# VectorE's order at a head's end in a two-layer hybrid attention block: the last score tile's normalisation placed before the next head's copies

## The chip, the cores and the metric

One Trainium2 chip, one of its cores. The whole network step is one program. The metric is the device time of one execution in microseconds (us): the median of several runs. A profile of one execution stands beside it.

## What is computed

Two layers, run over two sets of tokens at once: 512 latent tokens and 128 context tokens, 1024 wide. Everything is in float32. From the reference, cut to what matters here:

```python
def layer(x, cond, lp, cache=None, ropes=None):
    ...
    h = rmsnorm(x, lp['norm1']) * (1 + sc1) + sh1
    proj = h @ lp['w_in']
    ...
    y_a = gb * conv3(gc * xa, lp['conv_a'])
    ...
        y_b = blocked_attention((q_mla_rot, q_mla_raw), (k_l, k_x), (v_l, v_x), MLA_SCALE)
        y_c = blocked_attention((group_heads(axial_rope(qc, rope64), GQA_KV_HEADS), group_heads(qc, GQA_KV_HEADS)),
                                (axial_rope(kc, rope64), kc_x), (vc, vc_x), ATTN_SCALE)
        y_d = windowed_attention(group_heads(axial_rope(qd, rope64), SWA_KV_HEADS), axial_rope(kd, rope64), vd,
                                 group_heads(qd, SWA_KV_HEADS), kd_x, vd_x, lp['swa_sink'], ATTN_SCALE)
    ...
    y = jnp.concatenate([y_a, y_b, y_c, y_d], axis=-1) @ lp['w_out']
    x = x + g1 * y
    h = rmsnorm(x, lp['norm2']) * (1 + sc2) + sh2
    u = conv3(h @ lp['w_up'], lp['conv_ff'])
    ua, ub = jnp.split(u, 2, axis=-1)
    x = x + g2 * ((jax.nn.silu(ua) * ub) @ lp['w_down'])
    return x, new
```

There are three kinds of softmax attention with 4 heads each. Latent queries attend to the latent keys and to 128 cached ones, context queries to the 128 context keys. One kind sees a window of keys and has a sink, a logit that joins the softmax's denominator. Shift, scale and gate (sh, sc, g) come from a product of the conditioning with `w_ada` (adaLN).

## The kernel before

Each layer runs through the input projection, attention, the output projection and the feed-forward part. Large products are made of three float32r products of high and low halves (`H_hi`, `H_lo` for activations, `W_hi`, `W_lo` for weights). The queues of the five engines are written out by hand and meet at semaphores; an engine works strictly in its own order.

**Attention** goes by heads 0 to 11. Heads 0 to 3 are of the second kind above (y_c), 4 to 7 the windowed one with the sink, 8 to 11 the first kind (y_b). A head has five query tiles of 128: 0 to 3 latent, tile 4 context. `attention_order` (L173) writes one list of steps, and each engine walks it and takes its part:

- `("T", key)`: TensorE transposes something into PSUM bank 4 or 5, in turn, and another engine copies it out (`evac_fill`, L477). Keys of a head ("K", two parts, into `KTR`) and its queries ("Q", two parts, into `QTR`) are copied by VectorE, as are the fills of the first kind's projections ("MT", "MQ", "MV", into `CQ`, `PMG`, `PMS`, `KS`). Probabilities ("P", into `PT`) are copied by ScalarE. A transposition waits until the bank's last content but one has been copied out.
- `("S", h, q)`: TensorE makes the scores of tile q. VectorE takes the maximum (`maximum`, L1821), ScalarE the exponentials and their sum (`PR`, L945), VectorE divides (`normalise_probs`, L1835): a reciprocal and a multiplication of `PR` with it, and before them, in heads 4 to 7, an addition of the sink's term.
- `("V", h, k)`: TensorE multiplies `PT` with the values. When a head's output is complete, ScalarE writes its high half (`H_hi`) and VectorE its low half (`H_lo`, L1873).
- `("ADA", n)`: TensorE multiplies two half blocks of `w_ada`, each of 512 KB, which SyncE's queue brings into one of three buffers (`RW`), loaded again when the block before has been used.

The list interleaves two heads: while head h's scores are made, head h-1's probabilities are transposed and multiplied. Between two heads it reads:

```python
        if h == 0 or kv_of(h) != kv_of(h - 1):
            order += [("T", ("K", kv_of(h), 0)), ("T", ("K", kv_of(h), 1))]
        order += late + [("T", ("Q", h, 0)), ("T", ("Q", h, 1))]
        ...
        order += [("ADA", todo[0])] + t[:1]
        for q in range(NQ):
            order.append(("S", h, q))
            order += t[q + 1:q + 2] + v[q:q + 1]
```

`late` is the last value product of the head before h-1, and `t[:1]` the transposition of head h-1's tile 4, which waits for all five normalisations of that head (`s_norm`). Keys are shared by two heads in heads 0 to 7, so `KTR` is written anew behind heads 1, 3 and 5, and behind 8, 9 and 10. Behind head 7 there are no scores to interleave: the fills of the last group's projections come in, then head 7's transpositions and value products, then keys and queries of head 8. Behind head 11 follow the adaLN result's move and selection ("MOVE", "SEL") and the output projection.

VectorE (L1849 to L1858) normalises a tile one step late: after the maximum of tile q it divides tile q-1. The last tile's turn comes where the list has that head's first "P" transposition. ScalarE makes a tile's exponentials one step late too: those of tile 4 behind the copy of the head before's last probabilities.

Of the kernel before, what the change touches and what calls it, by code (L numbers as in the profile page):

```python
# [29 lines left out]
QT = NLAT // P  # L30
# [206 lines left out]
def by_scalar(key):  # L237

    return key[0] == "P"
# [19 lines left out]
def backbone_program(nc, x_prompt, x_sample, cache_mla_ckv, cache_mla_kpe, cache_gqa_k, cache_gqa_v,  # L259
# [5 lines left out]
    with ctx:  # L265
# [187 lines left out]
        def prob_ap(h, q):  # L453

            c0 = q * (P + NLAT)
            if q == QT:
                return PR[:, h % 2, c0:c0 + P]
            if h // 4 == 1:
                lo, hi = window(h, q)
                return PR[:, h % 2, c0:c0 + P * (1 + hi - lo)]  # L460
            return PR[:, h % 2, c0:c0 + P + NLAT].rearrange("p (b n) -> p b n", n=HALFK)

        def y_parts(k, r0):

            if k == TT:
                return [(r0, 0, CTX0, CTX0 + P)]
            return [(HD * x, QHALF * x, QHALF * x, QHALF * (x + 1)) for x in range(2)]
# [7 lines left out]
        def evac_fill(eng, copy, l, key):  # L476
# [5 lines left out]
            kind = key[0]  # L482
            if kind == "P":
                _, h, k = key
                i = 6 * h + P_SEQ.index(k)
                if i >= 2:
                    values_done(eng, l, i - 2)
                c0, c1 = (0, P) if k == TT else (P * queries(h, k)[0], P * queries(h, k)[1])
                copy(PT[:, i % 2, c0:c1], bank[:, c0:c1]).then_inc(done, 1)
            elif kind == "Q":  # L490
                _, h, part = key
                if h >= 2:
                    eng.wait_ge(s_mm, l * NS_ + NQ * (h - 1))
                c0, c1 = (0, NLAT) if part == 0 else (NLAT, NLAT + P)
                copy(QTR[:, h % 2, c0:c1], bank[:, 0:c1 - c0]).then_inc(done, 1)
            elif kind == "K":
                _, kv, part = key
                if kv >= 2:
                    last = max(h for h in range(HEADS) if kv_of(h) == kv - 2)
                    eng.wait_ge(s_mm, l * NS_ + NQ * (last + 1))  # L500
                c0, c1 = (0, 512) if part == 0 else (512, KEYS)
                copy(KTR[:, kv % 2, c0:c1], bank[:, 0:c1 - c0]).then_inc(done, 1)
            elif kind == "MT":
                i = key[1]
                if i >= 2:
                    eng.wait_ge(tr_mm, l * NFILL + (FILL_AT[("MV", i - 2)] + 1))
                else:
                    eng.wait_ge(rot_q, l * 3 + 2)
                if i < TT:
                    copy(CQ[0:96, i % 2, 0:2, :], bank[0:96, 0:2 * P].rearrange("p (k n) -> p k n", n=P))  # L510
                copy(CQ[:, i % 2, 2, :], bank[:, 2 * P:3 * P]).then_inc(done, 1)
            elif kind == "MQ":
                eng.wait_ge(new_out, l * 96 + 96)
                copy(PMG[:, key[1], 0:384], bank[:, 0:384]).then_inc(done, 1)
            else:
                src = bank.rearrange("p (h n) -> p h n", n=P)
                copy(KS[:, key[1], :, 0:HD], src[:, :, 0:HD])
                eng.wait_ge(new_out, l * 96 + 96)
                eng.wait_ge(raw_q, l * 3 + 2)
                i = key[1]  # L520
                dst = PMG[:, 0:4, 384:384 + HD] if i == PAST else \
                    PMS[:, i, 0:4 * HD].rearrange("p (h n) -> p h n", n=HD)
                copy(dst, src[:, :, HD:P]).then_inc(done, 1)
# [1038 lines left out]
        def _(dve):  # L1562
            v = nc.vector

            def copy(dst, src):
                return v.tensor_copy(dst, src)  # L1566
# [125 lines left out]
            for l in range(DEPTH):  # L1692
# [128 lines left out]
                def maximum(h, q):  # L1821
                    g, j = divmod(h, 4)
                    n = SIDX[(h, q)]
                    dve.wait_ge(s_mm, l * NS_ + (n + 1))
                    mx, nb = ST[:, 0, n % 4:n % 4 + 1], ST[:, 1, n % 4:n % 4 + 1]
                    s = score_ap(h, q, n)
                    v.tensor_reduce(mx, s, mybir.AxisListType.XY if len(s.shape) == 3 else AXX,  # L1827
                                    ALU.max).then_inc(s_max, 1)
                    dve.wait_ge(s_max, l * NS_ + (n + 1))
                    if g == 1:  # L1830
                        v.tensor_scalar(nb, mx, -SCALES[g], SK[:, j:j + 1], ALU.mult, ALU.min).then_inc(s_nb, 1)
                    else:
                        v.tensor_scalar(nb, mx, -SCALES[g], None, ALU.mult).then_inc(s_nb, 1)

                def normalise_probs(h, q):  # L1835
                    n = SIDX[(h, q)]
                    dve.wait_ge(s_exp, l * NS_ + (n + 1))
                    den, rec = ST[:, 2, n % 4:n % 4 + 1], ST[:, 3, n % 4:n % 4 + 1]
                    if h // 4 == 1:
                        dve.wait_ge(s_sink, l * 20 + (n - 20 + 1))  # L1840
                        v.tensor_tensor(den, den, SE[:, n % 4:n % 4 + 1], ALU.add).then_inc(s_den, 1)
                        dve.wait_ge(s_den, l * 20 + (n - 20 + 1))
                    v.reciprocal(rec, den).then_inc(s_rec, 1)
                    dve.wait_ge(s_rec, l * NS_ + (n + 1))
                    pr = prob_ap(h, q)
                    v.tensor_scalar(pr, pr, rec, None, ALU.mult).then_inc(s_norm, 1)  # L1846

                waiting = None
                for e in ORDERS[l]:  # L1849
                    if e[0] == "S":  # L1850
                        maximum(*e[1:])
                        if waiting:
                            normalise_probs(*waiting)
                        waiting = e[1:]
                        continue
                    if e[0] == "T" and e[1][0] == "P" and waiting and waiting[0] == e[1][1]:
                        normalise_probs(*waiting)
                        waiting = None  # L1858
                    if e[0] == "T" and not by_scalar(e[1]):
                        evac_fill(dve, copy, l, e[1])  # L1860
                    elif e == ("PREP", 2):

                        dve.wait_ge(tr_mm, l * NFILL + (FILL_AT[("K", 3, 1)] + 1))
                        for t in range(QT):
                            copy(KS[:, t, :, HD:96],
                                 PMM[:, t, 320:352].rearrange("p (o n) -> p o n", o=1).to_broadcast([P, 4, ROPE]))
                        v.memset(KS[:, PAST, :, HD:96], 0.0).then_inc(rot_k, 1)
                    elif e[0] == "V" and e[2] in (TT, QT):
                        h, k = e[1:]
                        yi, r0, tile = 3 * h + (k != TT), HD * (h % 2), YTILE[h // 4] + h % 4 // 2  # L1870
                        for x, (p0, b0, c0, c1) in enumerate(y_parts(k, r0)):
                            dve.wait_ge(y_hi, l * (3 * HEADS) + (yi + x + 1))
                            v.tensor_tensor(H_lo[r0:r0 + HD, tile, c0:c1], PS[p0:p0 + HD, 6, b0:b0 + c1 - c0],  # L1873
                                            H_hi[r0:r0 + HD, tile, c0:c1].bitcast(F32),
                                            ALU.subtract).then_inc(y_lo, 1)
# [280 lines left out]
```

## Time and profile before

| | us |
|---|---|
| median of 3 runs | 1832.27 (1827.96 to 1833.47) |
| the profiled execution | 1827.39 |
| its span, first to last instruction | 1825.6 |
| busy in it: TensorE matmul | 1714.5 (94%), 11625 instructions |
| VectorE | 1115.0 (61%), 2279 |
| ScalarE | 625.6 (34%), 1257 |
| GpSimd | 148.7 (8%), 152 |
| mean granted TensorE clock | 0.979 of full |

Times are counted from the first instruction. Attention in the first layer lies between 183 and 403, in the second between 1071 and 1281. In the rows, PE is TensorE's matmul, PEld its weight load, DVE VectorE, ACT ScalarE; L12 is line 12 of the kernel. L1106 is every product, L1110 every transposition, L1566 every copy of VectorE, L781 every copy of ScalarE, so a row is told by its tiles: what it writes stands left of the arrow.

### The profile page before, as it was taken

The numbers are of one execution on the slowest core, as the hardware profiler recorded it, in microseconds if no ns is written. First come the engines' busy times: TensorE is split into PE (matmuls) and PEld (weight loads), VectorE is DVE, ScalarE is ACT, GpSimd is POOL, SyncE is SP. The second block draws the span as 40 slices with busy tenths as digits, with TensorE's granted clock in tenths as the row PEclk, the third lists the DMA queues.
The fourth block names the chain that finished last, engine by engine and source line by source line (L and its number), as shares of the span: only waits on it lengthen the run. The fifth ranks groups of instructions, "written<-read, shape, count | busy, mean of one in ns | idle before, by whom it ended". The sixth has DMA issues, their size and how long they took to land.

```text
span 1825.6 us, 30070 instructions
## 1 busy us (share of the span) xinstructions
PE 1714.5 (94%) x11625; PEld 1539.5 (84%) x11625; DVE 1115.0 (61%) x2279; ACT 625.6 (34%) x1257; POOL 148.7 (8%) x152
## 2 busy tenths in 40 slices
PE   5899898899999999999989989878999999999997
PEld 3899554469999999999989965545999999999997
DVE  3656665555765655656782856656477556565675
ACT  2421553453432222232242235435343222222223
POOL 0351100020000000000004402010200000000000
PEclk7999999989999999999999999999999999999998
DMA  8431542332122222222312322212313222222211
GB/s 270 115 96 36 169 138 71 116 105 81 59 81 75 75 71 78 69 80 70 94 49 66 94 77 93 93 42 75 104 56 95 75 76 69 76 74 73 77 58 59
DMA packets 188438, 156.53 MB, mean 86 GB/s; under 512 B 7824, under 2 KB 175284, under 8 KB 188340
## 3 DMA queue, kind: packets, MB, share of 16 engines
q1 hardware_dynamic: 188340, 155.19, 27.7%
q8 instruction: 65, 1.06, 0.2%
q14 instruction: 33, 0.27, 0.1%
HBM read 151.86 MB, written 3.31 MB: 85 GB/s over the span
## 4 chain that ended last, share of the span: by engine, by line
PE 85%; DVE 7%; DMA 2%; ACT 2%; issue 2%; POOL 1%; SPq 0%; DVEq 0%; ACTq 0%
PE PS L1106 81%; PE PS L1110 4%; DMA RW<-in_w_ada_dram 1%; DMA RW<-in_w_in_dram 1%; DVE QTR L1566 1%; DVE H_lo L1873 1%; DVE H_lo L1627 1%; POOL SS L762 1%; ACT H_hi L781 1%; DVE PR L1846 1%; DVE X L1676 0%; POOL W_lo L740 0%; DVE ST L1827 0%; DVE XN_b L1614 0%; ACT PT L781 0%
## 5 line engine op out<-in xcount | busy, mean ns | idle before, releaser
L1106 PE MATMUL PS<-H_hi,W_lo 128*128 128x384 f32 (+1 forms) x1728 | 417.4, 310 | 0.0
L1106 PE MATMUL PS<-H_hi,W_hi 128*128 128x384 f32 (+1 forms) x1728 | 417.3, 310 | 0.0
L1106 PE MATMUL PS<-H_lo,W_hi 128*128 128x384 f32 (+1 forms) x1728 | 417.0, 310 | 0.0
L1106 PEld LDWEIGHTS PS<-H_lo,W_hi 128*128 128x128 f32 x1728 | 276.2, 189 | 0.0
L1106 PEld LDWEIGHTS PS<-H_hi,W_hi 128*128 128x128 f32 x1728 | 275.3, 189 | 1.1 <-issue 1.1
L1106 PEld LDWEIGHTS PS<-H_hi,W_lo 128*128 128x128 f32 x1728 | 276.1, 189 | 0.0
L781 ACT ACTIVATE W_hi<-RW 128x1024 fp32r<-128x1024 f32 (+1 forms) x176 | 183.9, 1049 | 190.0 <-PE PS L1106 161.4
L1942 DVE TENSOR_SCALAR CF<-U,VT 128x644 f32<-128x644 f32 x88 | 49.0, 556 | 268.8 <-ACT U L781 268.5
L1106 PE MATMUL PS<-G_hi,W_hi 128*128 128x384 f32 (+1 forms) x704 | 171.7, 310 | 0.0
L1106 PE MATMUL PS<-G_lo,W_hi 128*128 128x384 f32 (+1 forms) x704 | 171.4, 310 | 0.0
L1106 PE MATMUL PS<-G_hi,W_lo 128*128 128x384 f32 (+1 forms) x704 | 170.6, 308 | 0.0
L781 ACT ACTIVATE U<-PS 128x384 f32<-128x384 f32 (+1 forms) x176 | 67.4, 435 | 288.4 <-PE PS L1106 288.4
L1639 DVE TENSOR_TENSOR W_lo<-RW,W_hi 128x1024 fp32r<-128x1024 f32 x136 | 165.7, 1218 | 0.5 <-ACT W_hi L781 0.4
L1971 DVE TENSOR_TENSOR DN<-PS,DN 128x384 f32<-128x384 f32 (+1 forms) x288 | 122.0, 482 | 19.9 <-PE PS L1106 19.9
L1827 DVE TENSOR_REDUCE ST<-PS 128x1 f32<-128x640 f32 (+3 forms) x120 | 79.6, 664 | 88.5 <-PE PS L1106 88.2
L1106 PE MATMUL PS<-KTR,QTR 128*128 128x320 f32 (+3 forms) x432 | 127.2, 415 | 6.1 <-ACT PR L945 6.1
L1106 PE MATMUL PS<-W_hi,H_hi 128*128 128x256 f32 (+1 forms) x400 | 118.0, 295 | 13.6 <-DVE H_lo L1627 4.3
L781 ACT ACTIVATE PT<-PS 128x128 f32<-128x128 f32 (+2 forms) x144 | 73.2, 508 | 168.3 <-PE PS L1110 168.1
L1106 PE MATMUL PS<-W_lo,H_hi 128*128 128x256 f32 (+1 forms) x400 | 116.8, 292 | 0.0
L1106 PE MATMUL PS<-W_hi,H_lo 128*128 128x256 f32 (+1 forms) x400 | 116.6, 292 | 0.0
L740 POOL TENSOR_TENSOR W_lo<-RW,W_hi 128x1024 fp32r<-128x1024 f32 (+1 forms) x40 | 94.2, 2371 | 249.0 <-ACT W_hi L781 249.0
L1106 PEld LDWEIGHTS PS<-G_hi,W_lo 128*128 128x128 f32 x704 | 113.0, 189 | 0.0
(170 smaller groups left out, 2397.3 us busy)
## 6 DMA issues: line engine op xcount, KB each, us to landing
RW<-in_w_ada_dram SPq DMA_DIRECT2D x96, 512.0 KB, 4.5
RW<-in_w_up_dram SPq DMA_DIRECT2D x88, 512.0 KB, 3.8
RW<-in_w_down_dram SPq DMA_DIRECT2D x44, 512.0 KB, 3.6
RW<-in_w_in_dram SPq DMA_DIRECT2D x28, 512.0 KB, 3.7
RW<-in_w_out_dram SPq DMA_DIRECT2D x16, 512.0 KB, 3.4
RW<-in_w_in_dram SPq DMA_DIRECT2D x8, 352.0 KB, 3.0
out_dram<-OUT SPq DMA_DIRECT2D x5, 512.0 KB, 3.1
XIN<-in_x_sample_dram SPq DMA_DIRECT2D x4, 512.0 KB, 6.6
```

The source lines that it names most:

```text
L740: nc.gpsimd.tensor_tensor(lo[:, 0:width], RW[:, RAW_POS[("w", l, s)] % RAW, 0:width], hi[:, 0:width].bitcast(F32), ALU.subtract).then_inc( ...
L762: nc.gpsimd.tensor_tensor(SS[:, 1, 0:40], SS[:, 0, 0:40], K[:, K_MH:K_MH + 40], ALU.pow).then_inc(hp, 1)
L781: return nc.scalar.activation(dst, src, ACT.Copy)
L1106: return nc.tensor.matmul(out, lhsT, rhs, start=start, stop=stop, skip_group_check=True)
L1110: return nc.tensor.transpose(out, in_, K[0:n, K_ID:K_ID + n])
L1566: return v.tensor_copy(dst, src)
L1627: ins = v.scalar_tensor_tensor(H_lo[:, t, c0:c0 + b1 - b0], XN[x][:, t % 3, b0:b1], MOD[:, 24 * w + t, cond:cond + 1], H_hi[:, t, c0:c0 + ...
L1639: v.tensor_tensor(lo[:, 0:width], RW[:, raw, 0:width], hi[:, 0:width].bitcast(F32), ALU.subtract).then_inc(w_lo, 1)
L1827: v.tensor_reduce(mx, s, mybir.AxisListType.XY if len(s.shape) == 3 else AXX, ALU.max).then_inc(s_max, 1)
L1846: v.tensor_scalar(pr, pr, rec, None, ALU.mult).then_inc(s_norm, 1)
L1942: v.tensor_scalar(CF[:, ch, s, :], U[:, ch, s, 0:T], column(0), None, ALU.mult).then_inc(cv_own, 1)
L1971: ins = v.tensor_tensor(out, piece_bank(2 * t + x, x), out, ALU.add)
```

## The change

In VectorE's walk through the list, when the maximum of tile 4 (`QT`) has been taken and tile 3 divided, tile 4 is divided too, at once.

```diff
@@ -1852,6 +1852,9 @@
                         if waiting:
                             normalise_probs(*waiting)
                         waiting = e[1:]
+                        if e[2] == QT:
+                            normalise_probs(*waiting)
+                            waiting = None
                         continue
                     if e[0] == "T" and e[1][0] == "P" and waiting and waiting[0] == e[1][1]:
                         normalise_probs(*waiting)
```

The lists of the other engines stay as they are. VectorE, at the end of head 1 in the first layer, from tile 3's normalisation to head 2's first maximum, before:

```order
L1843 RECIPROCAL ST<-ST 128x1 [waits s_exp]
L1846 TENSOR_SCALAR PR<-PR,ST 128x640 [waits s_rec]
L1566 COPY KTR<-PS 128x512 [waits tr_mm]
L1566 COPY KTR<-PS 128x256 [waits tr_mm]
L1873 TENSOR_TENSOR H_lo<-PS,H_hi 64x256 [waits y_hi] x2
L1566 COPY QTR<-PS 128x512 [waits s_mm,tr_mm]
L1566 COPY QTR<-PS 128x128 [waits s_mm,tr_mm]
L1843 RECIPROCAL ST<-ST 128x1 [waits s_exp]
L1846 TENSOR_SCALAR PR<-PR,ST 128x128 [waits s_rec]
L1827 TENSOR_REDUCE ST<-PS 128x1 [waits s_mm]
```

and in the changed kernel, where line 1873 has become 1876:

```order
L1843 RECIPROCAL ST<-ST 128x1 [waits s_exp]
L1846 TENSOR_SCALAR PR<-PR,ST 128x640 [waits s_rec]
L1843 RECIPROCAL ST<-ST 128x1 [waits s_exp]
L1846 TENSOR_SCALAR PR<-PR,ST 128x128 [waits s_rec]
L1566 COPY KTR<-PS 128x512 [waits tr_mm]
L1566 COPY KTR<-PS 128x256 [waits tr_mm]
L1876 TENSOR_TENSOR H_lo<-PS,H_hi 64x256 [waits y_hi] x2
L1566 COPY QTR<-PS 128x512 [waits s_mm,tr_mm]
L1566 COPY QTR<-PS 128x128 [waits s_mm,tr_mm]
L1827 TENSOR_REDUCE ST<-PS 128x1 [waits s_mm]
```

The reciprocal and the multiplication of the 128 wide tile, which waits for ScalarE's exponentials (`s_exp`), have moved past the copies of the next keys, the two low halves of y and the copies of the next queries.

TensorE at the same place, in both kernels: the next head's queries, its adaLN products, the transposition of head 1's tile 4 and head 2's first score.

```order
L1110 MATMUL PS<-K,QS 128x128 [waits tr_ev_4]
L1110 MATMUL PS<-K,QS 128x128 x3
L1110 MATMUL PS<-K,QS 128x128 [waits tr_ev_5]
L1106 MATMUL PS<-RW,CT 32x256 [waits raw_in0]
L1106 MATMUL PS<-RW,CT 32x256 x3
L1106 MATMUL PS<-RW,CT 32x256 [waits raw_in1]
L1106 MATMUL PS<-RW,CT 32x256 x3
L1110 MATMUL PS<-K,PR 128x128 [waits s_norm,tr_ev_4]
L1106 MATMUL PS<-KTR,QTR 128x320 [waits tr_ev_4,tr_ev_5,s_exp]
```

Nothing moved here. `s_norm` counts the normalisations, `tr_ev_4` and `tr_ev_5` the copies out of the two banks, `raw_in` the landed weights.

VectorE at the end of head 7, before, from tile 3's normalisation on (the copies between are those of the last group's keys, values and queries):

```order
L1846 TENSOR_SCALAR PR<-PR,ST 128x384 [waits s_rec]
L1566 COPY KS<-PS 128x4x64 [waits tr_mm]
L1566 COPY PMS<-PS 128x256 [waits raw_q,new_out]
L1566 COPY CQ<-PS 128x128 [waits tr_mm]
L1566 COPY PMG<-PS 128x384 [waits new_out,tr_mm]
...
L1867 MEMSET KS 128x4x32
L1841 TENSOR_TENSOR ST<-ST,SE 128x1 [waits s_sink,s_exp]
L1843 RECIPROCAL ST<-ST 128x1 [waits s_den]
L1846 TENSOR_SCALAR PR<-PR,ST 128x128 [waits s_rec]
L1873 TENSOR_TENSOR H_lo<-PS,H_hi 64x256 [waits y_hi] x2
```

In the changed kernel the three rows from `ST<-ST,SE` on stand directly behind the first row, ahead of all of these copies.

## Rows read from the trace of the kernel before

**Rows 1.** Waits of the whole span: who waited for whom: us in total, times, longest.
```profile
PE PS L1110 <- DVE PR L1846: 29.2, 22, 2.7
```
**Rows 2.** Timeline, end of head 1, layer 0: start, us, engine, instruction [idle before].
```profile
204.20 0.20 ACT L945 ACTIVATION_READ_ACCUMULATOR PR<-PS,ST 128x1 f32 x1
204.63 1.02 DVE L1566 COPY KTR<-PS 128x512 f32<-128x512 f32 x2 [0.47 <-PE PS L1110]
205.93 0.88 DVE L1873 TENSOR_TENSOR H_lo<-PS,H_hi 64x256 fp32r<-64x256 f32 x2 [0.28 <-ACT H_hi L781]
206.07 1.07 PE L1106 MATMUL PS<-RW,CT 128*32 128x256 f32 x16
206.84 0.89 DVE L1566 COPY QTR<-PS 128x512 f32<-128x512 f32 x2
207.84 0.29 DVE L1846 TENSOR_SCALAR PR<-PR,ST 128x128 f32<-128x128 f32 x1
208.27 0.30 PE L1110 MATMUL PS<-K,PR 128*128 128x128 f32 x1 [1.13 <-DVE PR L1846]
208.50 1.31 PE L1106 MATMUL PS<-KTR,QTR 128*128 128x320 f32 x4
```
**Rows 3.** Timeline, end of head 2, layer 0.
```profile
221.24 0.88 DVE L1873 TENSOR_TENSOR H_lo<-PS,H_hi 64x256 fp32r<-64x256 f32 x2 [1.14 <-ACT H_hi L781]
222.14 0.89 DVE L1566 COPY QTR<-PS 128x512 f32<-128x512 f32 x2
...
224.22 1.31 PE L1106 MATMUL PS<-KTR,QTR 128*128 128x320 f32 x4
```
**Rows 4.** Timeline, end of head 4, layer 0.
```profile
253.86 0.89 DVE L1566 COPY QTR<-PS 128x512 f32<-128x512 f32 x2
...
255.84 0.89 PE L1106 MATMUL PS<-KTR,QTR 128*128 128x128 f32 x4
```
**Rows 5.** Timeline, end of head 5, layer 0.
```profile
267.30 1.02 DVE L1566 COPY KTR<-PS 128x512 f32<-128x512 f32 x2
...
269.47 0.89 DVE L1566 COPY QTR<-PS 128x512 f32<-128x512 f32 x2
...
271.36 0.89 PE L1106 MATMUL PS<-KTR,QTR 128*128 128x128 f32 x4
```
**Rows 6.** Timeline of TensorE, end of head 0, layer 0.
```profile
191.91 0.64 PE L1106 MATMUL PS<-RW,CT 128*32 128x256 f32 x8 [1.97 <-DMA RW<-in_w_ada_dram]
```
**Rows 7.** Timeline, end of head 8, layer 0.
```profile
341.41 1.01 DVE L1566 COPY KTR<-PS 128x512 f32<-128x512 f32 x2
...
342.84 1.07 PE L1106 MATMUL PS<-RW,CT 128*32 128x256 f32 x16
...
344.27 0.30 PE L1110 MATMUL PS<-K,PR 128*128 128x128 f32 x1 [0.35 <-DVE PR L1846]
```
**Rows 8.** Timeline, end of head 7, layer 0 and layer 1.
```profile
317.38 0.45 PE L1110 MATMUL PS<-K,PR 128*128 128x128 f32 x1 [2.49 <-DVE PR L1846]
...
317.86 0.28 ACT L781 ACTIVATE PT<-PS 128x128 f32<-128x128 f32 x1 [1.02 <-PE PS L1110]
...
318.97 0.78 ACT L781 ACTIVATE H_hi<-PS 64x256 fp32r<-64x256 f32 x2 [0.83 <-PE PS L1106]
...
1203.75 0.28 ACT L781 ACTIVATE PT<-PS 128x128 f32<-128x128 f32 x1 [1.04 <-PE PS L1110]
...
1204.39 0.78 ACT L781 ACTIVATE H_hi<-PS 64x256 fp32r<-64x256 f32 x2 [0.36 <-PE PS L1106]
```
**Rows 9.** Timeline of ScalarE, end of head 11, layer 0.
```profile
391.01 0.28 ACT L781 ACTIVATE PT<-PS 128x128 f32<-128x128 f32 x1 [1.38 <-PE PS L1110]
```
**Rows 10.** Stretches behind heads 7, 11, 11: busy by engine, granted clock, DMA share, GB/s.
```profile
317.30:328.50 11.20, 10.41 (x36) 4.46 (x36) 1.14 (x3) 3.65 (x9) 4.38 (x16) 0.55 0.00 0
390.60:402.70 12.10, 11.35 (x51) 6.71 (x51) 0.30 (x1) 5.80 (x10) 4.66 (x2) 0.58 0.28 88
...
1273.50:1280.90 7.40, 6.76 (x47) 3.91 (x47) 0.29 (x1) 5.48 (x10) 3.99 (x2) 1.00 0.06 8
```

## The prediction

> **What bounds the kernel now.** Heads are numbered 0 to 11, tiles 0 to 4, as in the code; "PE" is TensorE, "DVE" VectorE, "ACT" ScalarE. I read the waits of the whole span first: TensorE's transpositions of PR wait for the PR that VectorE writes 22 times, 29.2 us in all, 2.7 at most [rows 1]. With 12 heads in each of two layers that is one wait per head end but for two. So the question is what else has to be done at a head's end. For that I read the timeline there, engine by engine.
>
> Head 1 [rows 2] is the pattern. The exponential of its last tile is complete at 204.40 (204.20 + 0.20). VectorE copies KTR from 204.63, then H_lo, then QTR until 207.73 (206.84 + 0.89), and only then writes the last PR, complete at 208.13. TensorE's adaLN products end at 207.14; it stands 1.13 us, transposes PR at 208.27 and starts the next head's first score at 208.50. Its order is fixed, so this score stands behind the transposition though it needs only KTR and QTR. The reader is to see that PR could have been ready some 3 us earlier, and that the score, once PR no longer holds it, has QTR to wait for, which ends 0.77 before 208.50. The gain is therefore not the 1.13 of the wait.
>
> **The change, part by part.** No instruction is added or dropped. At every head end the reciprocal and multiplication of tile 4 (with the sink's addition in heads 4 to 7) move ahead of the next head's copies, on VectorE alone; no DMA and no other queue is touched. What is new is that the KTR, H_lo and QTR copies now stand behind a wait for the last exponential, and TensorE's transpositions of the next queries, with the adaLN products behind them, wait for the KTR copies.
>
> Release times I take from [rows 2]: from PR's end, 208.13, to the transposition 0.14; so the score starts 0.15 after the last thing it needs. The moved pair takes 0.47: 0.40 after the QTR copies, and they overlap their end a little; I take 0.5.
>
> *Heads 1, 3, 9 and 10, KTR copies, no sink.* The pair can start at 204.46 and ends at 204.93. The KTR copies were idle 0.47 before they began at 204.63, so they move by 0.3, to an end at 205.96. H_lo began at 205.93 after an idle 0.28, waiting for ACT; that slack swallows nearly all, 0.06 is left. QTR ends at 207.79. The adaLN products end at 207.14 + 0.33 = 207.47, still ahead. The score starts at 207.94 in place of 208.50: 0.56 a head, 8 heads, **4.5 us**.
>
> *Head 2, no KTR copies, no sink.* VectorE was idle 1.14 before H_lo at 221.24 [rows 3], that is from 220.10. In head 1 the exponential ends 0.24 after the third tile's PR; with the same here the pair takes 220.40 to 220.87 and hides entirely. QTR ends at 223.03 as before, the score starts at 223.18, not 224.22: 1.04, two layers, **2.1 us**.
>
> *Heads 4 and 6, no KTR copies, sink.* QTR ends at 254.75, the score started at 255.84 [rows 4]: 0.94 by the same reckoning. With the sink's addition the pair takes 0.65, and head 6 has less room before H_lo; I take 0.85 for the four, **3.4 us**.
>
> *Head 5, KTR copies and sink.* The KTR copies began at 267.30 with no idle time long enough to be listed [rows 5], so they move by about 0.57. Part is swallowed before H_lo, 0.36 reaches QTR: 270.36 + 0.36 + 0.15 = 270.87 in place of 271.36. I take 0.45, two layers, **0.9 us**.
>
> *Heads 0 and 8.* In head 0 TensorE's second adaLN product waited for its weights until 191.91 [rows 6] and ended at 192.55, which the change does not touch: 0. In head 8 KTR begins at 341.41 without a pause, the adaLN products end at 343.91 and the transposition waited only 0.35 more, to 344.27 [rows 7]. The copies move by 0.45, the queries' transpositions and the products with them, to 344.36, and the score starts about when it did: **0**.
>
> *Head 7.* Here 12 more copies and a memset (the next group's keys, values and queries) stood ahead of the pair, and TensorE stood 2.49 [rows 8]. ACT was idle 1.02 before its PT copy and 0.83 before its H_hi copies; in layer 1 it was 1.04 and 0.36. Both waits were for TensorE, which can now transpose as soon as the last product is out. ACT's own copies of QS and KS then come last. The chain on from there (H_lo, the next value product) moves by the sums, 1.85 and 1.40: **3.3 us**.
>
> *Head 11.* The same with ACT idle 1.38 before its PT copy [rows 9]; the later steps follow it one after another. Both layers: **2.8 us**.
>
> The sum is 4.5 + 2.1 + 3.4 + 0.9 + 0 + 3.3 + 2.8 = 17.0 us. Inside a head nothing moves: its first score starts earlier, and the rest follows from it on TensorE. Behind attention the output projection waits for the last value products, so the gain goes through to the end. The bounds: all of the 29.2 us [rows 1] on one side; on the other, each boundary term halved, since 0.15 of release and 0.3 to 0.57 of pushed copies are of the size of the gain, and head 7 and 11 kept: 5.5 + 6.1 = 11.5.
>
> The sum is made against the profiled execution: 1827.39 (span 1825.6), so 1810.4. That execution is the fastest of four; the median of the three runs is 1832.27, 4.9 above it. Reckoned from there it would be 1815.3. I put it between, **1813.0 us**. Some 0.3%, or 5.5 us, is what a measurement of this kernel can tell from no change.
>
> **The clock.** TensorE's granted clock fell to half after two of the waits that the change shortens: 0.55 in the stretch behind head 7's, 0.58 in that behind head 11's in layer 0 [rows 10]. Behind head 11's in layer 1 the same work ran at 1.00. It took 12.1 us in the one and 7.4 in the other, so that fall cost 4.7. In the stretch from 317.30, 10.41 busy at 0.55 would be 5.7 at full clock, at most 4.7 less, some 3 when the copies between set the pace. Since the same step of the program was followed by a fall in one layer and by none in the other, I leave the clock out of the sum. The Trainium skill (TensorE: Matmul & The Clock Gate, section "HAM oscillation — how this bites in real kernels") says that waits of TensorE between short bursts bring its clock back down and that the work behind them then starts cold; by that rule shorter waits would give back these falls too, and the sum would be 25 and not 17. Of the three places in [rows 10] two agree with it and one does not.
>
> **The rivals.**
>
> *The clock stays up.* What shortens the waits also removes the falls behind them: 17.0 + 4.7 + 3 = 24.7, so 1805. For it: the falls stand directly behind the longest head-end waits. Against: layer 1's end, and that other waits remain near head 7 (ACT's copies). Chance 0.15.
>
> *The weights set the pace.* Each head consumes adaLN weights; where these land just in time, as at head 0 (1.97 us of waiting [rows 6]), an earlier head end is only a longer wait for them. If that held at all boundaries, 10.9 us of the sum would go and the 6.1 of heads 7 and 11 would stay: 1824. Against it: at heads 1 and 8 the products ran without such a wait [rows 2, 7]. Chance 0.12 for much of it, and 0.06 that with that, or because something other than QTR holds the score, less than 5.5 us in all is left.
>
> *Slower: VectorE stands for ACT ahead of the copies.* The pair needs the last exponential, and ACT makes it behind a PT copy of the head before. Until now a late exponential cost nothing, since four to six instructions stood ahead of the pair; now KTR, H_lo and QTR stand behind it, and TensorE's transpositions and products behind KTR. An exponential that ends 1.0 later than at head 1 puts 1.0 + 0.5 on the copies and takes off the 1.13 of the wait: 0.37 at each of 22 boundaries, 8 us, 1838. It decides where the exponential ends over 0.6 later than the 204.40 of [rows 2]: from there what is pushed exceeds the 0.56 won at head 1. For it: head 8, with a slack of 0. Against: at head 1 VectorE was idle 0.47 and 0.28 on the way, without KTR copies 1.14 [rows 3], and nothing in the change makes ACT later. Chance 0.03.
>
> *It does not do what it says*: if the exponential came after all the copies, the pair would move in name only. At 204.40 it is ahead of them; this has no chance of its own.
>
> **How the numbers follow.** Forecast 0.64 (1813, own range 1807 to 1820), clock 0.15 (1805), weights 0.12 (1824), under 5.5 us 0.06, slower 0.03. Eight times in ten: 1803 to 1822. Faster by over 0.3% holds the first three, 0.91; within 0.06; slower 0.03.
>
> **What would show it.** In the changed profile the wait of the PR transpositions for PR should fall from 29.2 us to under 3. In its place some 5 to 10 us of short waits for QTR should stand before the first score or the PR transposition. At head 1 the score should start 0.15 after QTR's end and 0.5 to 0.6 earlier after the third tile's PR than now; at head 2 about 1.0 earlier; at heads 0 and 8 no earlier. PR of tile 4 should directly follow the one of tile 3. A wait for adaLN weights that grows by over 3 us would show the rival of the weights; KTR copies that start over 0.6 later, the slower one. I am wrong if attention (first score to the output projection) gets shorter by less than 5 us a layer with the clock as now.

## The result and the profile after

| | before | changed |
|---|---|---|
| median of the runs | 1830.38 us (1827.96 to 1833.47, 4 runs) | 1808.15 us (1807.27 to 1809.95, 4 runs) |
| profiled execution, its span | 1827.39, 1825.6 | 1807.65, 1805.9 |

The ratio is 0.9884, with a 95% interval of 0.9864 to 0.9904: 22 us less by the medians, 19.7 by the spans. The 2.5 between these two are spread: the profiled execution lay 3.0 under its median before, and 0.5 under it in the changed kernel. The forecast was 1813.0 with a range of 1803 to 1822.

The page of the changed kernel, its busy times and the granted clock in 40 slices:

```profile
span 1805.9 us, 30070 instructions
...
PE 1712.2 (95%) x11625; PEld 1537.8 (85%) x11625; DVE 1114.8 (62%) x2279; ACT 626.3 (35%) x1257; POOL 150.2 (8%) x152
...
PEclk7899999999999999999999999999999999999998
```

As many instructions as before, and nearly the same busy times; what went is idle time of TensorE, and some of its time at half clock. A *fall* is in what follows a stretch in which the granted clock stands at half. The view of waits of the changed kernel, first those of the weight loads, then those of the matmuls (who waited for whom: us in total, times, longest):

```profile
PEld PS L1106 <- DMA RW<-in_w_ada_dram: 27.1, 18, 3.6
...
PEld PS L1110 <- DVE QTR L1566: 12.5, 18, 1.0
```
```profile
PE PS L1106 <- DMA RW<-in_w_ada_dram: 17.3, 13, 2.7
PE PS L1110 <- DVE KTR L1566: 11.4, 16, 2.2
...
PE PS L1106 <- DVE H_lo L1876: 6.3, 8, 1.9
...
PE PS L1110 <- DVE QTR L1566: 3.9, 12, 0.5
...
PE PS L1110 <- DVE PR L1846: 0.6, 2, 0.3
```

The 29.2 us of waiting for PR [rows 1] have become 0.6, that is 28.6 less. Three other rows took some of it over. The matmuls' waits for QTR, of which before had none, are 3.9. Those for KTR, behind the pushed key copies, were 8.6 before and are 11.4. Those for H_lo (line 1873 before) were 3.0 and are 6.3. That is 10.0 in all, so 18.6 of the 28.6 are won. The weight loads' waits for QTR, 17.9 before, are 12.5. The waits for adaLN weights, 17.2 and for their loads 26.8 before, did not grow.

Timeline of the changed kernel, end of head 1, layer 0, against [rows 2] (start, us, engine, instruction, idle before):

```profile
208.06 0.20 ACT L945 ACTIVATION_READ_ACCUMULATOR PR<-PS,ST 128x1 f32 x1
208.49 0.29 DVE L1846 TENSOR_SCALAR PR<-PR,ST 128x128 f32<-128x128 f32 x1
208.69 1.02 DVE L1566 COPY KTR<-PS 128x512 f32<-128x512 f32 x2
209.43 0.77 PE L1110 MATMUL PS<-K,QS 128*128 128x128 f32 x5 [0.19 <-DVE KTR L1566]
209.79 0.88 DVE L1876 TENSOR_TENSOR H_lo<-PS,H_hi 64x256 fp32r<-64x256 f32 x2
210.13 1.07 PE L1106 MATMUL PS<-RW,CT 128*32 128x256 f32 x16
210.70 0.89 DVE L1566 COPY QTR<-PS 128x512 f32<-128x512 f32 x2
211.44 0.33 PE L1110 MATMUL PS<-K,PR 128*128 128x128 f32 x1 [0.24 <-DVE QTR L1566]
211.80 1.31 PE L1106 MATMUL PS<-KTR,QTR 128*128 128x320 f32 x4
```

The span has an offset of some 4 us here; what counts are differences. From the exponential's end (208.26 here, 204.40 before) the KTR copies start after 0.43 in place of 0.23, H_lo after 1.53 as before, QTR after 2.44 as before, and the score after 3.54 in place of 4.10. The score starts 0.21 after QTR's end. The same at head 2 of the changed kernel, against [rows 3]:

```profile
224.53 0.88 DVE L1876 TENSOR_TENSOR H_lo<-PS,H_hi 64x256 fp32r<-64x256 f32 x2 [0.38 <-ACT H_hi L781]
225.44 0.89 DVE L1566 COPY QTR<-PS 128x512 f32<-128x512 f32 x2
...
226.54 1.31 PE L1106 MATMUL PS<-KTR,QTR 128*128 128x320 f32 x4
```

From H_lo to the score 2.01 in place of 2.98. VectorE's idle time before H_lo is 0.38, not 1.14: the pair lies in it.

**By head end.** I measured each boundary in both traces, from the last maximum of a head to the first of the next (line 1827). What it got shorter by, layer 0 and layer 1 added, against the terms of the prediction:

| heads | forecast | measured |
|---|---|---|
| 1, 3, 9, 10 | 4.5 | 4.8 |
| 2 | 2.1 | 1.95 |
| 4, 6 | 3.4 | 3.15 |
| 5 | 0.9 | 1.15 |
| 0 | 0 | 0 at full clock |
| 8 | 0 | 0.33 |
| 7 | 3.3 | 2.5, and 1.7 of clock |
| 11 | 2.8 | 2.4, and 4.2 of clock |
| sum | 17.0 | 16.3, and 5.9 of clock |

Behind head 11 the stretch goes on to the output projection. "Of clock" is what is left where the granted clock differs. At head 7 the stretches got 2.18 and 2.01 shorter; a second run of the change, with as much half clock behind layer 1's head 7 as before, gave 1.01 there, and a run that leaves head 7 alone got 0.62 shorter in layer 0 by its clock only, so I take 1.5 and 1.0 for the wait. At head 11 layer 1 ran at full clock in both kernels and gained 1.2; I take the same for layer 0, where before has no such stretch at full clock. The split at head 7 is an estimate. Two experiments below that keep its wait, set against runs without it and with 6.8 us at half clock at the same place, give 1.2 and 1.6 for layer 0 and 0.8 to 1.2 for layer 1.

### The profile page after: what moved, and what is told of

The parts are those of the page before. It is cut to its first block, busy times and chain, and to the rows that moved or that the text cites. A ratio compares the mean times of both kernels' runs of the same rounds, so it can differ in the third digit from the quotient of the medians.

```text
span 1805.9 us, 30070 instructions
## 1 busy us (share of the span) xinstructions
PE 1712.2 (95%) x11625; PEld 1537.8 (85%) x11625; DVE 1114.8 (62%) x2279; ACT 626.3 (35%) x1257; POOL 150.2 (8%) x152
## 4 chain that ended last, share of the span: by engine, by line
PE 85%; DVE 6%; DMA 3%; ACT 3%; issue 2%; POOL 1%; SPq 0%; DVEq 0%; ACTq 0%
PE PS L1106 81%; PE PS L1110 4%; DMA RW<-in_w_ada_dram 2%; DMA RW<-in_w_in_dram 1%; DVE H_lo L1627 1%; POOL SS L762 1%; DVE H_lo L1876 1%; DVE QTR L1566 1%; DVE X L1676 0%; ACT PT L781 0%; DVE ST L1827 0%; ACT H_hi L781 0%; POOL W_lo L740 0%; DVE XN_b L1614 0%; DVE KTR L1566 0%
## 5 line engine op out<-in xcount | busy, mean ns | idle before, releaser
L1106 PEld LDWEIGHTS PS<-KTR,QTR 128*128 128x128 f32 x432 | 69.6, 193 | 54.0 <-issue 28.9
```

The costliest lines, as they stand in the source:

```text
L1106: return nc.tensor.matmul(out, lhsT, rhs, start=start, stop=stop, skip_group_check=True)
```

## The experiments

All times stand beside runs of the kernel before on the same chip. What an experiment changes is shown against the changed kernel.

**Only the two long waits: heads 7 and 11.**

```diff
-                        if e[2] == QT:
+                        if e[2] == QT and e[1] in (7, 11):
```

> The early normalisation only behind heads 7 and 11; at the other ten boundaries of a layer it stays behind the copies. Theory (each boundary gives what the first score is released earlier): the changed kernel gained 2.18 and 2.01 behind head 7 and about 1.2 each behind head 11 at full clock, so 6.6 us of the whole are kept, ratio to before about 0.996, 1823 to 1825 us; the transpositions' wait for PR stays near 21 us. Rival (the whole is the clock, which no longer falls behind the two longest waits): with these two waits gone nearly all of the 22 us are here, ratio 0.990 or less.

**All but these two.** The same line with `not in (7, 11)`.

> The complement: early normalisation everywhere but behind heads 7 and 11. Theory: 5.8 us in layer 0 and 5.6 in layer 1 are kept (sum of the boundaries measured in the changed kernel), 11.4 in all, ratio about 0.994, 1818 to 1820 us; the wait for PR falls to about 9 us (2.5 and 2.65 behind head 7, 1.95 twice behind head 11). Rival (the clock is the gain): ratio 0.997 or more and a half clock again behind heads 7 and 11. Rival (the weights set the pace): the waits for adaLN weights grow by what the boundaries lose.

The waits for PR of the first and of the second:

```profile
PE PS L1110 <- DVE PR L1846: 20.2, 19, 1.6
```
```profile
PE PS L1110 <- DVE PR L1846: 8.9, 4, 2.5
```

With the two alone: 1818.53 us, ratio 0.9937 (0.9917 to 0.9958). Without them: 1817.99, 0.9928 (0.9907 to 0.9949). Each is about half. The second came as expected. The first came 4.5 us under its range, which had the clock behind head 11 at nothing: its boundaries are 3.2 and 0.7 shorter at head 7, 5.4 and 1.2 at head 11, 10.5 in all. In it, heads 1 to 6 and 8 to 10 are as in the kernel before to 0.04 us where the clock is full; head 0 of layer 0 and head 8 of layer 1, with falls at or near them, are 1.4 and 0.8 longer. In the second, heads 1 to 6 are those of the whole change to 0.03 (0.57, 0.98, 0.56, 0.85, 0.67, 0.69 shorter than before, layer 0). So the terms are independent of each other, as the sum assumed. The totals do not add up as well: by medians 12.0 + 12.5 = 24.5 against 22, by spans 5.2 + 8.7 = 13.9 against 19.7. What differs from run to run is the clock, below.

**The pair made longer.** A multiplication of the last tile's PR by 1.0 goes ahead of the pair; the values stay the same.

```diff
+                    if q == QT:
+                        v.tensor_scalar(prob_ap(h, q), prob_ap(h, q), 1.0, None, ALU.mult)
```

> As the changed kernel, but tile 4 is first multiplied by 1.0, one more VectorE multiplication of 0.29 us ahead of every early normalisation. Theory: it costs its full length only where KTR copies follow (heads 1, 3, 5, 8, 9, 10: 12 boundaries, 3.5 us), nothing behind heads 2, 4 and 6, where VectorE stood idle over 1 us before H_lo (or at most 0.15 behind the sink heads), at most 0.3 behind head 7, nothing behind 0 and 11: 3.5 to 4.3 us over the changed kernel, ratio to before about 0.991. Rival (the pair is hidden everywhere): 0. Rival (VectorE's copies are the path at every boundary): 0.29 at 24 boundaries, 7 us.

1810.38 us, 0.989 (0.9867 to 0.9914). The span, 1808.9, is 3.0 more, but the boundaries hold only some 1.1 of it: nothing at heads 1, 2, 3 and 9, 0.13 each at 4, 5 and 6, 0.08 at 10, 0.04 to 0.12 at 7. Missed, and the VectorE rows of head 1 say why:

```profile
204.08 0.23 DVE L1840 TENSOR_SCALAR PR<-PR 128x128 f32<-128x128 f32 x1 [0.28 <-ACT PR L945]
204.23 0.16 DVE L1845 RECIPROCAL ST<-ST 128x1 f32<-128x1 f32 x1
204.42 0.29 DVE L1848 TENSOR_SCALAR PR<-PR,ST 128x128 f32<-128x128 f32 x1
204.62 1.02 DVE L1566 COPY KTR<-PS 128x512 f32<-128x512 f32 x2
```

The added instruction lasts 0.23 but only 0.15 passes until the next starts, and the pair itself moves the copies by 0.39 (204.23 to 204.62), not by 0.47. VectorE's rows overlap. Behind the KTR copies there was more slack than the 0.06 that I had left over: enough for this too.

**The pair between the copies.** At heads 1, 3, 5, 8, 9 and 10 it goes behind the second KTR copy, where VectorE waits for H_hi.

```diff
-                        if e[2] == QT:
+                        if e[2] == QT and e[1] not in (1, 3, 5, 8, 9, 10):
...
+                        if waiting and waiting[1] == QT and e[1][0] == "K" and e[1][2] == 1:
+                            normalise_probs(*waiting)
+                            waiting = None
```

> The changed kernel, but where KTR copies follow (heads 1, 3, 5, 8, 9, 10) tile 4 is normalised behind them and ahead of H_lo. Theory (the pair ahead of the keys hides in VectorE's idle time before the keys and before H_lo; behind the keys it pushes H_lo and QTR by 0.4): heads 1, 3, 9, 10 lose 0.35 each, head 5 about 0.2, head 8, where the keys had no idle time before them, wins 0.3: 2.6 us slower than the changed kernel. Rival (pushing the keys, with the queries' transpositions and the adaLN products behind them, is what costs): up to 3 us faster than the changed kernel.

1809.14 us, 0.9882 (0.9867 to 0.9898): no different from the change. VectorE at head 1:

```profile
204.06 0.15 DVE L1843 RECIPROCAL ST<-ST 128x1 f32<-128x1 f32 x1
204.25 0.28 DVE L1846 TENSOR_SCALAR PR<-PR,ST 128x128 f32<-128x128 f32 x1
204.45 0.87 DVE L1879 TENSOR_TENSOR H_lo<-PS,H_hi 64x256 fp32r<-64x256 f32 x2
205.35 0.89 DVE L1566 COPY QTR<-PS 128x512 f32<-128x512 f32 x2
```

The pair fits the idle time before H_lo here just as well as the idle time before KTR. Against the change heads 1, 3 and 9 are 0.01 to 0.04 worse, 10 is 0.14 to 0.17 worse, 5 lies between 0.14 worse and 0.04 better, and head 8 is 0.39 better. Both expectations were wrong for the whole. Of the theory's parts only the gain at head 8, where VectorE had no pause, came: 0.39, expected 0.3.

**The same order, another wait.** VectorE as before; TensorE takes the next head's first score ahead of tile 4's transposition.

```diff
-        order += [("ADA", todo[0])] + t[:1]
+        order += [("ADA", todo[0])]
...
-            order += t[q + 1:q + 2] + v[q:q + 1]
+            order += (t[:1] if q == 0 else []) + t[q + 1:q + 2] + v[q:q + 1]
...
-                        if e[2] == QT:
-                            normalise_probs(*waiting)
-                            waiting = None
```

> The kernel before with VectorE's program as it was, but TensorE makes the next head's first score ahead of the transposition of tile 4. Theory (only TensorE's order held the score; but VectorE then takes that score's maximum before it normalises tile 4): the score starts 0.56 earlier at head 1, yet the transposition waits for maximum, then the pair, until some 2.6 us later than before, so TensorE stands 1.6 instead of 1.1 with nothing left to do: about 1.2 us lost at each of 18 to 20 boundaries, 20 to 25 us slower than before, ratio 1.011 to 1.014. Rival (what counts is how early the first score starts): 9 to 11 us faster than before, ratio 0.995.

1876.21 us, 1.0249 (1.0231 to 1.0267): 46 slower, twice what was expected. The timeline behind head 1:

```profile
214.83 1.32 PE L1106 MATMUL PS<-KTR,QTR 128*128 128x320 f32 x4 [0.80 <-DVE QTR L1566]
216.18 0.82 DVE L1827 TENSOR_REDUCE ST<-PS 128x1 f32<-128x640 f32 x1 [1.56 <-PE PS L1106]
...
217.30 0.28 DVE L1846 TENSOR_SCALAR PR<-PR,ST 128x128 f32<-128x128 f32 x1
217.73 0.74 PE L1110 MATMUL PS<-K,PR 128*128 128x128 f32 x5 [1.59 <-DVE PR L1846]
```

The score does start earlier, and the boundary is as short as with the change. But on VectorE the pair now comes behind the score's maximum, which waits for the score, so TensorE waits 1.59 at the next step. From maximum to maximum inside a head it loses 1.89, but nothing in heads 0 and 8. The waits for PR, 29.2 before, are 41.2. Twenty heads at 1.89, less the 12.8 by which all boundaries together got shorter, are 25 us; I put the remaining 21 down to the clock: 99 us of the span between 100 and 1700 at half clock, against 37.5 before. So the exchange on TensorE alone does not pay. Exchange and early pair together were not run.

**Queries ahead of H_lo.** If QTR is what the score waits for, copying it ahead of H_lo must bring more. H_lo is held for heads 0 to 5 and 7 to 9 until the second query copy is out.

```diff
...
+                        if e[2] == QT and e[1] in LATE:
+                            held = e
+                        else:
+                            low_y(*e[1:])
+                    if held and e[0] == "T" and e[1][0] == "Q" and e[1][2] == 1:
+                        low_y(*held[1:])
+                        held = None
```

(`LATE = (0, 1, 2, 3, 4, 5, 7, 8, 9)`, `held = None` at first, and `low_y` holds the lines that made H_lo.)

> The changed kernel, and VectorE also copies the next head's queries (QTR) ahead of the two low halves of y (H_lo), behind heads 1 to 6, 9 and 10; behind head 7 the copies of head 8's keys and queries come ahead of H_lo. Theory (QTR's copies now release the next head's first score, and the low halves stand ahead of them for 0.9 us): the score comes earlier until the adaLN products bound it: about 0.45 at heads 1, 3, 9 and 10, 0.55 at head 2, 0.7 at 4, 0.25 at 5, 0.1 at 6, 0.8 behind head 7, so 4.2 us a layer, 8 us over the changed kernel, ratio to before 0.984 to 0.985, about 1801. Rival (the adaLN products, or ScalarE, release the score already): under 2 us. Rival (the low halves' delay holds the next value product, which waits for them): slower than the changed kernel.

1800.10 us, 0.9837 (0.9821 to 0.9852), and in the profile 12.2 less span than the change. Head 1:

```profile
207.65 0.89 DVE L1566 COPY QTR<-PS 128x512 f32<-128x512 f32 x2 [0.42 <-PE PS L1110]
207.66 1.07 PE L1106 MATMUL PS<-RW,CT 128*32 128x256 f32 x16
208.46 0.86 DVE L1852 TENSOR_TENSOR H_lo<-PS,H_hi 64x256 fp32r<-64x256 f32 x2
208.66 0.33 PE L1110 MATMUL PS<-K,PR 128*128 128x128 f32 x1
208.82 1.25 PE L1106 MATMUL PS<-KTR,QTR 128*128 128x320 f32 x4
```

QTR now ends at 208.54, and TensorE goes without a pause from the adaLN products (208.73) to the transposition and the score. The boundaries are another 0.57 shorter at 1, 3, 9 and 10, 0.3 to 0.85 at 2, 4, 5, 6 and 7, and 0 at 8: some 10 us, where 8 were expected. That QTR was what held the first score is shown by this, and also that the adaLN products are next.

**Both together:** queries first, and at heads 5 and 8 the pair behind the KTR copies (the diffs of the two experiments with `not in (5, 8)`).

> The kernel with the queries' copies ahead of the low halves, and behind heads 5 and 8 tile 4 normalised behind the KTR copies. Theory (there the keys had no idle time before them, so the pair ahead of them delays the queries' transpositions and the adaLN products): 0.39 at head 8 and 0.2 at head 5 in each layer, 1.2 us faster than with the queries first alone, too little for the times to tell, to be read from the trace; ratio to before 0.983. Rival (at head 8 something else releases the score): no change at head 8.

1796.34 us (1794.1 to 1800.43), 0.9826 (0.9799 to 0.9852): 12 below the change by medians, 11 by ratios, and the lowest median of the study, though the profiled span, 1795.7, is 2.0 over that of the experiment before. Over the experiment before, it wins 0.38 and 0.52 at head 5 and 0.39 at head 8; by total time the two can't be told apart.

**The clock.** Two runs ask for chance: the same two kernels once more.

> The kernel before once more, for a second profile. Theory (the half clock behind head 11 of layer 0 comes from the 1.95 us wait there, which the changed kernel does not have): a fall behind head 11 in layer 0 or 1 again, from head 11's first maximum to the output projection 23 to 26 us in the layer where it falls against 20.5 without, while every boundary in attention repeats the first profile's time to 0.05 us where the clock is full. Rival (that fall was chance): none behind head 11 in either layer, or falls elsewhere for as many us as in the changed kernel.

> The changed kernel once more, for a second profile and a closer ratio. Theory: ratio 0.988 to 0.990; from head to head the boundaries give the same times to 0.05 us as in the first profile wherever the clock is full, while the stretches at half clock lie elsewhere. Rival (the clock falls are part of the program): they lie at the same heads again.

The kernel before again: 1827.73, 0.9987 (0.9971 to 1.0003). The change again: 1811.99, 0.9895 (0.9869 to 0.9921). Where the clock repeats, the boundaries of heads 1 to 6 and 8 to 10 do too, most of them to 0.02 and all to 0.07 us. The six falls of the kernel before came back, each 0.5 to 0.6 later: 317.2, 392.3, 467.4, 958.9, 1068.2 and 1204.7 in its first profile. Of the change they came back less exactly (behind layer 1's head 7 one of 3.4 us became one of 6.8, and another of 6.8 came behind head 8), but behind head 11 there was none again. Then one wait at a time:

```diff
-                        if e[2] == QT:
+                        if e[2] == QT and e[1] in (11,):
```

> The early normalisation behind head 11 alone. Theory (the 1.95 us wait there brings a fall of TensorE's clock in layer 0, and without it the fall is gone): from head 11's first score to the output projection 20.8 in layer 0 in place of 26.2 and 19.3 in layer 1 in place of 20.5, so 6.6 us in all, of which 4.2 are the clock; ratio 0.996. Rival (the fall was gone in the other kernels because everything ahead of it had moved): 23 to 26 in layer 0, 2.4 us in all, ratio 0.999.

and with `in (7,)`:

> The early normalisation behind head 7 alone. Theory: boundary 7 gives 1.4 to 2.2 in each layer, as the clock there falls for one or two stretches of 3.4 us, the fall behind head 11 in layer 0 stays (23 to 26 from head 11's first score to the output projection): 3 to 5 us in all, ratio 0.997 to 0.998. Rival (moving what lies behind is enough to lose that fall): 20.8 there, 8 us in all, ratio 0.9955.

By total time head 11 alone is just told from no change, 1823.28, 0.9977 (0.996 to 0.9994), and head 7 alone is not, 1825.76, 0.9982 (0.9959 to 1.0005). Their traces say more. The stretches from head 11's last maximum to the output projection, in layer 0 and layer 1 (busy by engine, granted clock, DMA share, GB/s). Before:

```profile
386.98:402.71 15.73, 12.99 (x63) 7.27 (x61) 2.56 (x9) 7.51 (x15) 4.66 (x2) 0.67 0.41 134
...
1270.03:1280.93 10.90, 8.27 (x58) 4.31 (x56) 2.55 (x10) 7.47 (x17) 4.02 (x2) 1.00 0.04 7
```

Pair moved at head 7 only, so with the wait behind head 11 as before:

```profile
384.89:400.48 15.59, 13.04 (x64) 7.30 (x62) 2.56 (x9) 7.51 (x15) 4.66 (x2) 0.67 0.43 136
...
1268.80:1282.53 13.73, 11.10 (x58) 5.84 (x56) 2.56 (x10) 7.58 (x17) 4.66 (x2) 0.75 0.19 60
```

Pair moved at head 11 only:

```profile
389.62:399.99 10.37, 8.92 (x64) 4.91 (x62) 2.66 (x9) 7.40 (x15) 4.42 (x2) 1.00 0.40 125
...
1265.88:1275.60 9.72, 8.39 (x59) 4.31 (x57) 2.65 (x10) 7.47 (x17) 3.92 (x2) 1.00 0.04 8
```

The whole change:

```profile
382.87:393.24 10.37, 8.92 (x63) 4.91 (x61) 2.66 (x9) 7.41 (x15) 4.41 (x2) 1.00 0.39 126
...
1251.53:1261.25 9.72, 8.39 (x59) 4.31 (x57) 2.65 (x10) 7.48 (x17) 3.92 (x2) 1.00 0.02 7
```

All but 7 and 11, so with the wait behind head 11 as before, layer 0:

```profile
385.80:398.34 12.54, 10.33 (x63) 5.68 (x61) 2.56 (x9) 7.40 (x15) 4.67 (x2) 0.86 0.37 116
```

The first number behind the comma is TensorE's busy time: the 63 or 64 rows of work in layer 0 take 12.99 at a clock of 0.67 and 8.92 at 1.00. The wait for PR behind head 11 was 1.96 in both layers wherever VectorE has its old order there. Five profiles keep it: before twice, all but 7 and 11, 7 alone, and the score first. In these, 7 of 10 such stretches fell to half clock: all five of layer 0, and in layer 1 those of 7 alone and of the score first. In the eight that order VectorE so that PR comes first, 16 of 16 ran at 1.00, within 10.36 to 10.37 in layer 0 and 9.71 to 9.72 in layer 1. At full clock the wait is worth 10.90 − 9.72 = 1.18. Where the clock fell behind it, wait and fall together are worth 15.73 − 10.37 = 5.36 with 10.2 us at half clock, as in both profiles of before, but only 12.54 − 10.37 = 2.17 with 3.4.

Head 11 alone thus gives 5.36 + 1.18 = 6.5 by its stretches, as the theory had it (6.6), though everything ahead of it stayed as before. At head 7 alone, the boundary got 3.06 shorter in layer 0 and 1.00 in layer 1, neither within the expected 1.4 to 2.2; what the clock has in it is not shown by one profile.

## Why the prediction was right

**What bounds a head's end** was read right. The gain of a boundary is not the wait that goes but what is left of it until the next condition, here QTR. At head 1 the wait was 1.13 and the gain 0.56, as worked out. Queries first showed it from the other side.

**The waits' sum** came to 16.3 against 17.0, all of its terms within 0.35 but head 7's and 11's. That the sum is so close is in part luck: these two were put 1.2 too high, and heads 1, 3, 5, 8, 9 and 10 together 0.9 too low. The parts of a term were less exact than the term. The release took 0.21 where I had read 0.15 for PR, and the pushed KTR copies cost 0.21 where I took 0.3 and nothing reached QTR where I had left 0.06. These offset each other: luck too.

**Head 5** was 1.15 (0.67 and 0.48) against 0.9, since I let 0.36 of the pushed copies through to QTR and less came. **Head 8** gave 0.17 a layer against 0. The copies and the products behind them moved by 0.40 where I took 0.45, and the transposition and the score followed the products at once:

```profile
340.58 1.07 PE L1106 MATMUL PS<-RW,CT 128*32 128x256 f32 x16
341.58 0.33 PE L1110 MATMUL PS<-K,PR 128*128 128x128 f32 x1
```

**Head 7** is the largest miss among the waits: 3.3 forecast, 2.5 at equal clock. The term added ACT's idle times ahead of PT and H_hi. The timeline of the changed kernel shows what that left out:

```profile
314.35 0.33 PE L1110 MATMUL PS<-K,PR 128*128 128x128 f32 x1
...
316.28 0.26 ACT L781 ACTIVATE PT<-PS 128x128 f32<-128x128 f32 x1
316.44 0.77 ACT L781 ACTIVATE H_hi<-PS 64x256 fp32r<-64x256 f32 x2
316.83 0.87 DVE L1876 TENSOR_TENSOR H_lo<-PS,H_hi 64x256 fp32r<-64x256 f32 x2 [0.75 <-ACT H_hi L781]
...
317.85 0.66 PE L1106 MATMUL PS<-PT,PMS 128*64 128x128 f32 x2 [1.93 <-DVE H_lo L1876]
```

TensorE transposes PR without a wait, but ScalarE reaches that copy only behind its own of QS and KS, and TensorE then stands 1.93 for H_lo: the wait moved to the next engine. In layer 0 the 0.83 that ACT stood idle ahead of H_hi [rows 8] was in part a slow product; in the kernel before it reads

```profile
317.76 1.11 PE L1106 MATMUL PS<-PT,PMS 128*64 128x256 f32 x2
```

and in the changed one, at 314.61, the same product took 0.65. These 0.46 of clock I had counted as idle time: 1.85 − 0.46 = 1.39, against the 1.5 that I took as measured, between 1.2 and 1.6. Why layer 1 gave 1.0 and not 1.40 I did not follow up. **Head 11** was 1.2 a layer, where I took 1.4 from ACT's idle of 1.38 [rows 9].

**The rivals.** The weights did not set the pace: their rows stand as they were. The slower case did not come: the exponential was ahead of the copies and they moved by 0.2, not by over 0.6.

*The clock stays up* came about in part, and the step that left the clock out of the sum is the one that failed. By one fall behind head 11 and one non-fall I held the fall for chance. In layer 0 it was the wait's: with the wait all five stretches fell, without it none of eight, and moving the pair at head 11 alone was enough for that. That gave 4.2 us, where I had read 4.7 for the fall: the 12.1 and the 7.4 that I set against each other are not quite the same work, since at full clock layer 0's stretch is 0.65 longer (10.37 against 9.72). In layer 1 the same wait was followed by a fall in two of five, so the wait alone does not decide it. The fall behind head 7 is another matter. It got shorter (10.2 us at half clock to 6.8 in layer 0, 6.8 to 3.4 in layer 1), but with the wait kept (head 11 alone) it was 6.8 in layer 0 too and in layer 1; and the change run again had 6.8 in both layers. Over all thirteen profiles the fall of layer 0 lasts 10.2 twice and 6.8 three times with the wait, and 3.4 twice and 6.8 six times without it. That leans towards the change, but that its 1.7 us belong to it is not shown.

By spans the 19.7 are −1.5 ahead of attention's first score, 11.0 from there to the end of attention in layer 0, 2.8 between, 7.4 in attention of layer 1, and 0 behind; both layers are above the 5 us under which I had called myself wrong. 16.3 and 4.2 make 20.5; the 0.8 left over is the balance of other changes of the clock: behind head 7, at 467.4 and at 1068.2 falls got shorter or went, and at the start of attention (177.7 to 184.5, 194.8 to 198.2 and, in layer 1, 1072.0 to 1075.4) new ones came. The falls of layer 0's start are not the change's: they also stand in the profiles with only head 7 (178.3, 192.0) or only head 11 (180.2, 193.8) changed, whose program up to there is that of before, and are absent from two that have the change (the pair made longer, and the pair between the copies).

So the measured 1808 lies between the forecast's 1813 and the rival's 1805.
**The reference point.** I took a place between the profiled execution less the sum (1810.4) and the median less the sum (1815.3). The first would have been nearer.

**Open.** Where falls come that no edit explains: between 100 and 1700 us the profiles hold 37.5 us at half clock for the kernel before, both times, 27.3 and 37.5 for the changed one, 54.6 with head 7 alone and 30.7 with head 11 alone. The two of the changed kernel are some 10 us at half clock apart, about 4 of time by what 10.2 us of it cost behind head 11.

## What to carry to other kernels

Price a wait that you remove by what the waiting engine needs next, not by its length, and look for the copies that now stand behind the moved work: short dependent work hides in any idle time ahead of them. Once the first condition is gone, order the engine's list by who waits for each result; the queries ahead of H_lo brought about half as much again as this change. A wait that the clock falls behind costs more than it shows, here 2.2 to 5.4 us where it is worth 1.2 at full clock; one place that stays up is no reason to leave that out of the sum.

## What the runs showed of the hardware

- Small dependent instructions of VectorE cost less than their rows say, since a row can overlap the next: reciprocal and multiplication together moved the next copy by 0.39, where their rows are 0.16 + 0.29 = 0.45, and a further 128x128 multiplication took 0.15 to the next start with a row of 0.23 (the pair made longer, head 1).
- A single wait of 1.96 us behind head 11, in a program that keeps TensorE busy, was followed by a fall from 2.4 to 1.2 GHz in layer 0 in all five profiles that keep it and in layer 1 in two of five; without it the clock stayed at 1.00 in all 16 stretches.
- The same program up to a place can have other falls there: the kernel before had none at the start of layer 0's attention in either profile, and the kernel with only head 11 changed had two, of 3.4 us each.
- Exchanging two steps of TensorE, as easy to argue for as the change, cost 46 us, an estimated 25 of them at full clock and the rest with it at half.
